# Products of the identity that nobody reads, put on TensorE at the borders of stages, in a two-layer decoder step

## The reference, cut to what matters

```python
for l in range(DEPTH):                                   # DEPTH = 2
    g = norm_g[l]
    yp, state_p = (even_mixer_prompt | odd_mixer)(rmsnorm(xp, g[0]), ...)
    ys, state_s = (even_mixer_sample | odd_mixer)(rmsnorm(xs, g[0]), ...)
    xp += rmsnorm(yp, g[1]);  xs += rmsnorm(ys, g[1])
    xp += rmsnorm(cross_attend(rmsnorm(xp, g[2]), mk_p, mv_p, w_xq[l], w_xo[l]), g[3])    # and xs with its own memory
    xp += rmsnorm(square(relu(rmsnorm(xp, g[4]) @ w_ff1[l])) @ w_ff2[l], g[5])            # and xs
```

## Time and profile before

| | |
|---|---|
| device time, median of 3 runs | 3691.43 us (3685.84 to 3693.31) |
| the profiled execution, its own time | 3705.86 us |
| its span | 3704.0 us |
| TensorE busy (matmuls) | 3266.7 us, 88% of the span |
| DVE, ACT busy | 1822.9 us (49%), 1424.8 us (38%) |
| GpSimd busy | 170.8 us (5%) |
| mean granted clock of TensorE | 0.927 |

### The profile page before, as it was taken

How to read it: one execution, slowest core, us unless ns; L and a number is a source line. 1 busy time by engine, 2 the same in 40 slices (tenths; PEclk the granted TensorE clock), 3 DMA queues, 4 the chain that set the end, 5 groups by cost and what they waited for, 6 DMA issues and landing times. The chain is left out here.

```text
span 3704.0 us, 44376 instructions
## 1 busy us (share of the span) xinstructions
PE 3266.7 (88%) x17291; PEld 2601.8 (70%) x17291; DVE 1822.9 (49%) x3223; ACT 1424.8 (38%) x2408; POOL 170.8 (5%) x184
## 2 busy tenths in 40 slices
PE   8879994876988799999997999995988799999996
PEld 6725642444786799899785776673776699899885
DVE  5677997633335444444544330066335444444443
ACT  6452112632344433433444330263344433433443
POOL 0020200032000000000000000022000000000000
PEclk9989996998999899999998997866989899999998
DMA  3122121056020443333452101102031333434353
GB/s 102 25 70 76 40 83 67 1 196 226 22 104 29 142 137 114 128 123 127 135 159 74 33 26 35 35 1 79 1 114 41 129 127 116 135 115 135 126 159 104
DMA packets 226196, 341.91 MB, mean 92 GB/s; under 512 B 34375, under 2 KB 163119, under 8 KB 225988
## 3 DMA queue, kind: packets, MB, share of 16 engines
q1 hardware_dynamic: 214212, 297.13, 24.8%
q0 software_dynamic: 11776, 41.95, 3.5%
HBM read 328.56 MB, written 10.19 MB: 91 GB/s over the span
## 5 line engine op out<-in xcount | busy, mean ns | idle before, releaser
L635 DVE TENSOR_TENSOR s_mlp_w2l<-s_mlp_w2b,s_mlp_w2h 128x1024 fp32r<-128x1024 f32 x192 | 235.1, 1225 | 581.4 <-ACT s_mlp_w2h L521 581.4
L172 PE MATMUL ps<-s_mlp_xl,s_mlp_w1h 128*128 128x384 f32 (+1 forms) x1536 | 498.9, 325 | 10.2 <-DVE s_mlp_xl L653 10.2
L174 PE MATMUL ps<-s_mlp_xh,s_mlp_w1h 128*128 128x384 f32 (+1 forms) x1536 | 495.5, 323 | 0.0
L173 PE MATMUL ps<-s_mlp_xh,s_mlp_w1l 128*128 128x384 f32 (+1 forms) x1536 | 494.9, 322 | 0.0
L521 ACT CAST s_mlp_w2h<-s_mlp_w2b 128x1024 fp32r<-128x1024 f32 x192 | 201.5, 1050 | 585.5 <-PE ps L174 585.3
L172 PE MATMUL ps<-s_mlp_w2l,s_mlp_hh 128*128 128x512 f32 x1024 | 404.4, 395 | 20.4 <-DVE s_mlp_hl L672 16.2
L173 PE MATMUL ps<-s_mlp_w2h,s_mlp_hl 128*128 128x512 f32 x1024 | 402.3, 393 | 0.0
L174 PE MATMUL ps<-s_mlp_w2h,s_mlp_hh 128*128 128x512 f32 x1024 | 402.3, 393 | 0.0
L172 PEld LDWEIGHTS ps<-s_mlp_xl,s_mlp_w1h 128*128 128x128 f32 x1536 | 289.4, 188 | 42.1 <-issue 35.9
L173 PEld LDWEIGHTS ps<-s_mlp_xh,s_mlp_w1l 128*128 128x128 f32 x1536 | 289.5, 188 | 6.2
L174 PEld LDWEIGHTS ps<-s_mlp_xh,s_mlp_w1h 128*128 128x128 f32 x1536 | 289.2, 188 | 0.0
(11 more groups left out here) (558 smaller groups left out, 5691.7 us busy)
## 6 DMA issues: line engine op xcount, KB each, us to landing
s_mlp_w1b<-w_ff SPq DMA_DIRECT2D x96, 1024.0 KB, 6.2
s_mlp_w2b<-w_ff SPq DMA_DIRECT2D x96, 1024.0 KB, 8.4
x_kb<-cache_mem_k SPq DMA_DIRECT2D x16, 512.0 KB, 6.8
x_vb<-cache_mem_v SPq DMA_DIRECT2D x2, 4096.0 KB, 20.4
s_orows_raw<-w_in_odd SPq DMA_DIRECT2D x32, 256.0 KB, 2.9
s_convsel_w<-w_in_even SPq DMA_DIRECT2D x12, 512.0 KB, 3.9
x<-x_prompt SPq DMA_DIRECT2D x8, 512.0 KB, 5.6
ev_mixT<-w_in_even SPq DMA_DIRECT2D x16, 256.0 KB, 3.7
```

Of the source, the lines that this page charges most:

```text
L172: nc.tensor.matmul(out, ah, bl, start=first, stop=False, skip_group_check=True)
L173: nc.tensor.matmul(out, al, bh, start=False, stop=False, skip_group_check=True)
L174: return nc.tensor.matmul(out, ah, bh, start=False, stop=last, skip_group_check=True)
L635: nc.vector.tensor_tensor(w2l[:, s % RING], w2b[:, c % 3, s % FC, :], w2h.bitcast(F32)[:, s % RING], ALU.subtract).then_inc(low2, 1)
```

## The change

A helper issues `n` products of the 128 x 128 identity by the identity repeated four times (128 x 512, float32) into a PSUM bank that is free at that place. Nothing reads them, and nothing is signalled. TensorE's list gets them at nine places in the code: at the start of `stage_out` and behind its last tile (four stages each), at the start of `stage_mlp` and behind its first turns (two stages each), behind the last product of `mlp0`, at the end of `convsel`, at the start of `qkg` and of `mlstm`, and at the end of `mlstm`. That is 4 x 17 + 2 x 28 + 30 + 12 + 16 + 6 + 24 = 212 products. Two of the places get a wait ahead of them (for the bank).

```diff
+def keep_warm(nc, G, bank, n):
+
+    for _ in range(n):
+        nc.tensor.matmul(G.ps[:, bank, :].rearrange("p (a t) -> p a t", a=4), G.ident[:], bc(G.ident[:].unsqueeze(1), [P, 4, P]),
+                         start=True, stop=True)
@@ stage_out, tensor
                 pe.wait_ge(s_turned, 2)
+            keep_warm(nc, G, 2, 8)
             sample(0)
             sample(1)
...
                         turn(t + 1, k // 4)
+            pe.wait_ge(added, NT - RING + 2)
+            keep_warm(nc, G, 2 * (NT % RING), 9)
@@ stage_mlp, tensor
+            keep_warm(nc, G, 7, 20)
             for e in range(6):
                 turn(e, e)
+            keep_warm(nc, G, 7, 8)
             up(0)
...
                     down_sample(s)
+            if name == "mlp0":
+                keep_warm(nc, G, bank(), 30)
@@ stage_conv_select, tensor
                     ins.then_inc(tail_turned, 1)
+            keep_warm(nc, G, 4, 12)
@@ stage_qk_gates, tensor
+            keep_warm(nc, G, 7, 16)
             pe.wait_ge(side_in, 64)
@@ stage_mlstm, tensor
+            keep_warm(nc, G, 7, 6)
             pe.wait_ge(made, 2)
             stabilise(0)
...
             ins.then_inc(cout, 1)
+            pe.wait_ge(inter_kept, N)
+            keep_warm(nc, G, 3, 24)
```

## The result

The change made the kernel slower: 3725.17 us (median of 20 executions, 3721.6 to 3736.5) beside 3692.9 us for the kernel before (20 executions, 3682.5 to 3734.1), a ratio of 1.008 with a 95% interval of 1.0062 to 1.0099. The prediction was 3708 us, so the direction was right and the loss of 32 us about twice the 16.7 foretold. Two more numbers matter for what follows. The two profiled executions lie 21.2 us apart (3705.86 and 3727.05), not 32. And the kernel with the change repeats within 15 us where the kernel before spreads over 52. In what follows, medians and ratios leave out executions in a slow state (4909 us in `no_mlstm`, 7908 us in `ml_narrow`, and 6579, 3734 and 3734 us of the kernel before beside other runs).

A forecast was written before the change was run, and what follows sets the result against it. TensorE, busy 88% of the span, was taken to bound the kernel by its clock and idle stretches. Eight terms summed to +16.7 us, added to the 3691.4 us median: 3708 us, own range 3697 to 3722, wide range 3682 to 3740.

The forecast's parts named there:

- Term 1: Behind the four output projections: nine products outlast ACT's last square, each meeting 2.1 us late; +8.4 us.
- Term 2: At the two MLP entries: 20 and 8 products delay the first turns, less some clock regained; +14.2 us together.
- term 3: Behind `mlp0`: 30 products overrun the gap by 11.1 us, `orows` gives 1.2 us back; +9.9 us.
- Term 4: Behind `convsel`: 12 products take 12.2 us, 5.7 more than the gap, about 1.5 come back in `attend`; +4.2 us.
- Term 5: At the starts of the output projections: eight products, +2 us for `even_out`, +1 for the other three together; +3 us.
- Term 6: At the start of `qkg`: 16 products delay the gate products by 5.8 us, which give back 1 us; +4.8 us.
- Terms 7 and 8: Start of `mlstm`: six products keep its loop at the high clock, -28.8 us; behind `mlstm`: 24 products, `mlstms` gaining 2, +1 us.
- term 7: Start of `mlstm`: +2.8 us delay, loop 31.6 us shorter at the rate of its second stretch (the row); -28.8 us.
- The second: Rival: in `mlstm` the clock is not held, 31.6 us of gain are gone; +48.3 us, 3740 us, chance 0.17.
- The third: Rival: a product costs one record, so nearly all fills fit their gaps; 3655 us, chance 0.06.
- The first: Rival: fills lift the whole next stage, 26.7 us more back in `attend`, the gates and `orows`; 3681 us, chance 0.13.
- The fourth: Rival: some delays lie beside transfers that come late anyhow, the sum shrinks to within 0.2%; chance 0.12.

The follow-up runs named there:

- `no_mlstm`: The change without the 6 products at the start of `mlstm`, the other 206 kept: 3746.99 us, ratio 1.0146 to the kernel before.
- `ml_narrow`: The kernel before with only one fill, at the start of `mlstm`: 26 products of 16 columns in place of 6 of 512; 3713.91 us, ratio 1.0055.
- the second trace: Second profiled execution of the kernel before, unchanged: span 3679.7 us, `mlstm` 117.45 us; the run's time was 3690.81 us.

## Why the prediction was right in direction and short in size

**The terms, trace against trace.** The sum of +16.7 us is to be held against the 21.2 us between the profiled executions. Term 1: TensorE ends 2.2 us behind ACT at each of the four meetings, +8.8 (+8.4 foretold). Term 2: +6.0 in `mlp1` and, of `mlp0`'s 19.5, the 8.4 that aren't term 3's, 14.4 (14.2). Term 3: the meeting is 11.1 us late and `orows` gave 0.2 back, +10.9 (9.9; the 1.2 us to be regained there did not come). Term 4: +5.6 (4.2): the fill of `convsel` took 12.57 us as worked out, and the 1.5 us back in `attend` did not come. Term 5: +2.7 (3). Term 6: +2.0 (4.8): the delay is 5.9 us (5.8), but the gates gave back 4.7 us, not 1, since their first part kept the fill's clock; I had let the level drop at once (the other 0.8 us lie behind the gates). Terms 7 and 8: `mlstm` and `mlstms` -25.7 (-27.8): 29.8 us came out of the loop, 31.6 were expected. The last 2.5 us lie in stages that got no fill; single stages of these differ by 1 to 2 us between traces of the kernel before, so nothing is read from them. The Trainium skill, page "TensorE: Matmul & The Clock Gate", section "HAM oscillation — how this bites in real kernels", counts half of the throttled time as lost; by that estimate 39 us would have come out of the loop, and the row was the better guide.

**The step that failed** is the last one: "The profiled execution would become 3722.6 us, and the median 3691.4 + 16.7 = 3708 us". The first half was within 5 us (3727.05), the second was short by 17. The 14.4 us by which the profiled execution lay above the median were noted, and then the sum was added to the median as if they were spread over the kernel. They are the very stretch that term 7 undoes: a `mlstm` that stayed low for 78.1 us, while other executions of the same program have some 17 us of it. The change sets every execution to about 115.7 us of `mlstm`, so it takes 25.5 us from the profiled one and about 2 from one like the second trace. The median of before stands between: less the 1.9 us around the span and 3562 to 3568 us of other stages, 3692.9 leaves 123 to 129 us for `mlstm`, so there were 7 to 13 us to gain, not 25. Worked with that, the sum is 21.2 + 12 to 18 = 33 to 39 us; 32 were measured, 23 to 37 by the interval. That the direction came out is no luck, since a smaller gain in `mlstm` only makes the sum larger. That the time lies inside the wide range is in part: 3725 is 3 us above the forecast's own range of 3697 to 3722, which has no end for the base, and the wide one reaches 3740 only for a rival that did not happen. That `mlstm` took 123 to 129 us in the median execution is worked out, not seen in a trace; the traces of before show 117.3, 117.5 and 141.2.

**The rivals.** The second (the clock isn't held in `mlstm`) did not happen: six products hold it, in every trace that has them. The third (one record to a product) fell with the 424 records. The first fell with the gates and with `orows` at 0.58: the clock stayed only where the work behind the fill kept it, and the narrow products bear out that the gates' busy time told against it. The fourth (about no change) is out by the interval: the delays of terms 1 to 4 came in at or a little above the sizes foretold, so none of them was hidden.

What stays open is what sets the moment at which an untreated `mlstm` rises, at 17 us in two executions and at 78 in one. No run here varies that by itself. Open too is whether 16 columns or another trait of the narrow products (26 short ones, 52 records) is what loses the clock: only that one shape was tried.

## What to carry to other kernels

Before a change is costed at the stretch that it mends, see whether that stretch is the same in a second execution: a low-clock stretch whose length is chance inflates the gain by what one trace happens to show, and the trace's distance from the median is the first hint. A fill that ends when the next operand arrives costs nothing, one that ends later is a delay of the whole program wherever all engines meet; so count its records (two for a float32 product), divide the gap by their measured time and stay below it. And fill only where the work behind is able to keep the clock: here two wide products, in a wait at whose end the clock fell before, did that for the whole of `mlstm`, and thirty behind `mlp0` did next to nothing for the next stage.

## What the runs showed of the hardware that was not expected

One program's clock in one stage differed by 61 us of low time between executions, with nothing else changed. TensorE that is busy with products of 16 columns, for 9.8 us in the fill and 23.7 in the gates, did not gain or keep the high clock; four records of 512 columns (1.96 us) ahead of `mlstm` kept it through all 16 units, in which TensorE has 34 to 39 of every 40 us of work.
